# Causal attention inside a two-block layer stack: values as the stationary operand in two column halves, weights normalised before they are transposed

## The reference

```python
for blk in range(s // Q_BLOCK):
    q0, kend = blk * Q_BLOCK, (blk + 1) * Q_BLOCK
    sc = (jnp.einsum('bqhd,bkhd->bhqk', q_nope[:, q0:kend], k_nope[:, :kend])
          + jnp.einsum('bqhd,bkd->bhqk', q_rope[:, q0:kend], k_rope[:, :kend]))
    sc = sc.astype(jnp.float32) * scale
    qi = q0 + jnp.arange(Q_BLOCK)[:, None]
    ki = jnp.arange(kend)[None, :]
    sc = jnp.where(ki <= qi, sc, -jnp.inf)
    pr = jax.nn.softmax(sc, axis=-1).astype(v.dtype)
    outs.append(jnp.einsum('bhqk,bkhd->bqhd', pr, v[:, :kend]))
o = jnp.concatenate(outs, axis=1)
```

## Time and profile before

| | |
|---|---|
| median of 3 runs | 3857.33 us (3854.55 to 3866.11) |
| profiled execution, its own time | 3858.3 us |
| its span | 3856.6 us |
| mean granted TensorE clock | 0.955 of full |
| TensorE matmul busy | 3517.2 us, 91% of the span |
| VectorE / ScalarE / GpSimd busy | 63% / 41% / 29% of the span |
| the attention steps | from 2254 to 2794 us of the span |

### The profile page before, as it was taken

The page is one execution under the profiler, slowest core; times in us unless marked ns, Lnnn a source line. Parts: engine busy times, 40 slices in busy tenths (PEclk is TensorE's granted clock), DMA queues, the critical chain, the costliest instruction groups (busy, mean ns, idle before and its releaser), DMA issues. The chain is left out here.

```text
span 3856.6 us, 44384 instructions
## 1 busy us (share of the span) xinstructions
PE 3517.2 (91%) x16340; PEld 2784.6 (72%) x16340; DVE 2415.6 (63%) x2812; ACT 1580.0 (41%) x2196; POOL 1124.3 (29%) x675
## 2 busy tenths in 40 slices
PE   7899998595999999968989899999989889999998
PEld 3678887464788778756777667777767678878876
DVE  5569557636888888866655222222236488887778
ACT  4322234444777777735222222222232342234443
POOL 1232220234111111143321212222144355545552
PEclk9899999796999999989999999999989999999999
DMA  5312346556999999954421312112154524478854
GB/s 190 108 50 89 115 134 211 211 174 240 374 401 402 398 400 402 367 208 143 144 94 55 126 47 67 58 63 69 44 207 142 175 97 152 155 266 282 270 170 136
DMA packets 225591, 717.22 MB, mean 186 GB/s; under 512 B 26896, under 2 KB 62064, under 8 KB 209296
## 3 DMA queue, kind: packets, MB, share of 16 engines
q1 hardware_dynamic: 184000, 620.37, 44.5%
q10 hardware_dynamic: 31632, 64.80, 4.5%
q0 software_dynamic: 9792, 29.81, 2.0%
HBM read 574.00 MB, written 140.89 MB: 185 GB/s over the span
## 5 line engine op out<-in xcount | busy, mean ns | idle before, releaser
L100 PE MATMUL m_b<-b_high,m_high 128*128 128x512 f32 x960 | 406.0, 423 | 8.4 <-POOL m_low L2616 6.4
L102 PE MATMUL m_b<-b_high,m_low 128*128 128x512 f32 x960 | 383.7, 400 | 0.0
L101 PE MATMUL m_b<-b_rest,m_high 128*128 128x512 f32 x960 | 383.2, 399 | 0.0
L2614 POOL TENSOR_TENSOR m_high<-m_raw,m_one 128x1024 fp32r<-128x1024 f32 x60 | 119.9, 1998 | 782.8 <-PE m_b L102 712.7
L3904 POOL TENSOR_TENSOR t_wl<-t_buf,t_wh 128x512 fp32r<-128x512 f32 x136 | 195.1, 1439 | 240.8 <-ACT t_wh L4035 240.7
L2663 ACT ACTIVATE m_ob<-m_b 128x512 f32<-128x512 f32 x120 | 71.0, 596 | 400.5 <-PE m_b L102 364.8
L100 PE MATMUL zs_z<-zs_hs,zs_high 128*128 128x512 f32 (+1 forms) x584 | 226.5, 388 | 8.5 <-DVE zs_hs L310 8.0
L100 PEld LDWEIGHTS m_b<-b_high,m_high 128*128 128x128 f32 x960 | 185.9, 194 | 61.3 <-issue 12.0
L100 PE MATMUL t_b<-b_high,t_wh 128*128 128x512 f32 x544 | 214.6, 394 | 11.0 <-POOL t_wl L3904 11.0
L101 PEld LDWEIGHTS m_b<-b_rest,m_high 128*128 128x128 f32 x960 | 183.1, 191 | 49.4 <-issue 9.4
L101 PE MATMUL zs_z<-zs_hs,zs_high 128*128 128x512 f32 (+1 forms) x584 | 218.7, 375 | 0.0
(11 more groups left out here) (707 smaller groups left out, 9495.1 us busy)
## 6 DMA issues: line engine op xcount, KB each, us to landing
moe_raw<-in_expert_w SPq DMA_DIRECT2D x79, 2048.0 KB, 10.1
ex_raw<-in_expert_w SPq DMA_DIRECT2D x39, 2048.0 KB, 10.5
t_raw<-in_w_ff SPq DMA_DIRECT2D x192, 256.0 KB, 3.5
m_raw<-in_w_ug SPq DMA_DIRECT2D x60, 512.0 KB, 4.5
t_buf<-hid SPq DMA_DIRECT2D x112, 256.0 KB, 4.4
hid<-t_x SPq DMA_DIRECT2D x96, 256.0 KB, 2.3
yrows<-ex_y ACTq DMA_DIRECT2D x38, 512.0 KB, 11.2
gates<-m_ob SPq DMA_DIRECT2D x32, 512.0 KB, 2.9
```

The source lines that it names most:

```text
L100: nc.tensor.matmul(out, w[0], x[0], start=first, stop=False)
L101: nc.tensor.matmul(out, w[0], x[1], start=False, stop=False)
L102: return nc.tensor.matmul(out, w[1], x[0], start=False, stop=last)
L2614: g.tensor_tensor(W.high[j][:], W.raw[j][:], W.one[:].broadcast_to([P, D]), ALU.mult).then_inc(W.rounded, 1)
```

## The change

Values: the value tile of 64 columns is now the stationary operand and the turned weights move (128 columns). The output has channels on 64 partitions and queries along the row. Even key tiles add into one half of bank 4's partitions, odd key tiles into the other half (`part`, `rows`): two column halves of the array. ScalarE copies the odd half to `at_other` (`copy`), VectorE adds the even half to it into `at_yT`; block 0 has one tile and is only copied, by VectorE. `at_yT` is what is stored, so `pair` and its 32 turns are gone, and the store waits for VectorE's last addition.

Weights: the division by the sum moves ahead of the turns. A new VectorE step `weigh` takes the sum, its reciprocal, and scales `at_pr` in place, up to 128 by 1024. The turns of step n wait for it (`weighed`) and no longer for ScalarE's exponentials alone.

Filler: it is counted in quarters of a unit (2 steps, 6 matmuls): 2, 2, 3, 3, 4, 4, 4, 2 in the blocks of a head and 4 at its end, which is 7 units a head as before. In the state-space mixer each half became two quarters in the same place.

```diff
-        for k in range(KD) if part is None else range(part * KD // 2, (part + 1) * KD // 2):
+        for k in range(KD) if part is None else range(part * KD // 4, (part + 1) * KD // 4):
...
-        self.fills = [2 - b % 2 for b in range(self.QB)]
+        self.fills = [2, 2, 3, 3, 4, 4, 4, 2]
...
+    def rows(self, h):
+        return slice(h % 2 * VH, (h % 2 + 1) * VH)
+
+    def part(self, n, odd):
+
+        return self.ps[4][self.rows(n // self.QB + odd), n % 2 * P:(n % 2 + 1) * P]
...
-        def pair(p):
-            pe.wait_ge(self.taken, 16 * (p + 1))
-            for b in range(self.QB):
-                mm = turn(ps[2 + b // 4][:, b % 4 * P:(b % 4 + 1) * P], self.o[p % 2][:, b], C["ident"][:])
-            mm.then_inc(self.o_turned, 1)
...
-            pe.wait_ge(self.exped, n + 1)
+            pe.wait_ge(self.weighed, n + 1)
             pe.wait_ge(self.moved, self.T0[n])
-            pe.wait_ge(self.o_moved, h // 2 * 2)
...
-            F.halves(pe, self.fills[b])
+            F.quarters(pe, self.fills[b])
             pe.wait_ge(self.moved, self.T0[n + 1])
             pe.wait_ge(self.taken, n)
             for x in range(b + 1):
-                mm = mm_(ps[4][:, n % 2 * P:n % 2 * P + VH], self.pT[n % 2][:, x * P:(x + 1) * P], self.v[:, x, h * VH:(h + 1) * VH], start=x == 0, stop=x == b)
+                mm = mm_(self.part(n, x % 2), self.v[:, x, h * VH:(h + 1) * VH], self.pT[n % 2][:, x * P:(x + 1) * P], start=x < 2, stop=x + 1 >= b)
             mm.then_inc(self.summed, 1)
...
+        def copy(n):
+            if n % self.QB == 0:
+                return
+            act.wait_ge(self.summed, n + 1)
+            act.wait_ge(self.taken, n - 1)
+            S.activation(self.other[n % 2][self.rows(n // self.QB)], self.part(n, 1), ACT.Copy).then_inc(self.copied, 1)
...
             take(self.fills[b])
+            copy(n)
...
+        def weigh(n):
+            b, sm = n % self.QB, self.sm[n % 2]
+            dve.wait_ge(self.exped, n + 1)
+            if b >= 4:
+                st.then(V.tensor_tensor(sm[:, 0:1], sm[:, 0:1], sm[:, 1:2], ALU.add))
+            st.then(V.reciprocal(sm[:, 1:2], sm[:, 0:1]))
+            pr = self.pr[n % 2][:, 0:(b + 1) * P]
+            V.tensor_scalar(pr, pr, sm[:, 1:2], None, ALU.mult).then_inc(self.weighed, 1)
...
             if not last:
                 greatest(n + 1)
+                weigh(n + 1)
...
+            y = self.yT[p % 2][r, b * P:(b + 1) * P]
+            if b:
+                dve.wait_ge(self.copied, n - h)
+                V.tensor_tensor(y, self.part(n, 0), self.other[n % 2][r], ALU.add).then_inc(self.taken, 1)
+            else:
+                V.tensor_copy(y, self.part(n, 0)).then_inc(self.taken, 1)
```

More of the change, by code:

```diff
@@ L2620, in unit @@
     def unit(self, pe, *ms, part=None):
-        for m in ms if part != 1 else ():
+        for m in () if part else ms:
             if m % 2 == 0:
@@ L2642, in multiply, with quarters @@
             self.made += 1
-    def halves(self, pe, count):
-        for x in range(self.parts, min(self.parts + count, 2 * (self.total - self.made))):
-            self.unit(pe, self.made + x // 2, part=x % 2)
+    def quarters(self, pe, count):
+        for x in range(self.parts, min(self.parts + count, 4 * (self.total - self.made))):
+            self.unit(pe, self.made + x // 4, part=x % 4)
             self.parts += 1
     def settle(self):
-        self.made, self.parts = self.made + self.parts // 2, 0
+        self.made, self.parts = self.made + self.parts // 4, 0
     def take(self, act, count=1):
@@ L3068, in tensor @@
                 rows(i + 1)
-            self.F.halves(pe, 1)
+            self.F.quarters(pe, 2)
             pe.wait_ge(self.y_done, i + 1)
@@ L3167, in __init__ @@
         self.pr, self.pT = [q.sb(f"pr{j}", [P, SEQ]) for j in range(2)], [q.sb(f"pT{j}", [P, SEQ]) for j in range(2)]
-        self.o, self.yT = [q.sb(f"o{j}", [P, self.QB, P]) for j in range(2)], q.sb("yT", [P, SEQ])
+        self.other, self.yT = [q.sb(f"other{j}", [P, P]) for j in range(2)], [q.sb(f"yT{j}", [P, SEQ]) for j in range(2)]
         self.mx, self.sm = [q.sb(f"mx{j}", [P, 2]) for j in range(2)], [q.sb(f"sm{j}", [P, 2]) for j in range(2)]
@@ L3268, in tensor @@
                     key(h + 1)
-                if h % 2:
-                    pair(h // 2)
-                F.halves(pe, 2)
+                F.quarters(pe, 4)
                 if h + 1 < MH:
@@ L3316, in weigh, with store @@
             ins.then_inc(self.exped, 1)
[L3318 to L3325, removed]
+        def copy(n):
[4 more added lines that the diff above has]
+            S.activation(self.other[n % 2][self.rows(n // self.QB)], self.part(n, 1), ACT.Copy).then_inc(self.copied, 1)
+        def store(p):
+            act.wait_ge(self.taken, 16 * (p + 1))
+            act.dma_start(self.R["y"][p], self.yT[p % 2][:]).then_inc(self.stored, 16)
         F.take(act, 2)
@@ L3335, in take @@
             begun += parts
-            F.take(act, made + begun // 2 - F.moved)
+            F.take(act, made + begun // 4 - F.moved)
         for n in range(MH * self.QB):
@@ L3347, in scalar @@
             take(self.fills[b])
+            copy(n)
             if last:
-                if h % 2:
-                    pair(h // 2)
-                take(2)
+                take(4)
                 if h + 1 < MH:
@@ L3355, in scalar @@
                         weights(h + 2)
+                if h % 2:
+                    store(h // 2)
     def vector(self, dve):
@@ L3412, in vector @@
         greatest(0)
+        weigh(0)
         for n in range(MH * self.QB):
@@ L3417, in vector @@
                 greatest(n + 1)
+                weigh(n + 1)
             elif h + 1 < MH:
                 query(h + 1)
[L3420 to L3424 removed]
             dve.wait_ge(self.summed, n + 1)
[L3426 removed]
+            p, r = h // 2, self.rows(h)
             if h % 2 == 0 and p >= 2:
[L3428 to L3429 removed]
+                dve.wait_ge(self.stored, 16 * (p - 1))
+            y = self.yT[p % 2][r, b * P:(b + 1) * P]
[4 more added lines that the diff above has]
+                V.tensor_copy(y, self.part(n, 0)).then_inc(self.taken, 1)
             if last and h + 1 < MH:
```

9 lines of the change are left out of this document (2 added, 7 removed).

## The result

The changed kernel takes 3876.1 us (median of 12 runs, 3870.1 to 3881.1 without one run at 5915), the kernel before 3859.5 beside it (12 runs). The ratio is 1.0034 (95% interval 1.0027 to 1.0042): slower by 16.6 us, where 3856 us and no change were forecast. The time lies in the forecast's range, but the forecast's likeliest case is wrong. The profiled execution after took 3871.7 us, its span is 3870.0. In the span the stage of the 64 steps, from the start of the first turn to the last store of `at_yT`, grew from 538.7 us (2254.84 to 2793.58, the latter in the earlier trace rows) to 556.9 (2251.77 to 2808.68), by 18.2.

What follows compares the result with a forecast made beforehand. TensorE's queue bounds the 64 steps (527.4 of 540 us busy). Terms -2.4 - 2.7 - 1.9 + 4.2 + 1.2 = -1.6 us gave 3856 us, counted as no change; range 3842 to 3884 us.

Steps and rivals of the forecast that it cites:

- the forecast's likeliest case: Whole kernel: halves overlap, shape changes cost, inner scalings stay hidden; 3856 us, own range 3846 to 3866, 52%.
- Values: Value matmuls on TensorE: 61.9 us before, 59.5 after including shape changes, so -2.4 us.
- overlap of the halves: Value matmuls: even and odd key tiles run at once, 0.22 us a pair, 35.2 us for 160 pairs.
- price of the shape: Each step's switch between whole-array work and 64-column value tiles: 0.38 us in and out, 64 times, 24.3 us.
- Rivals 1 to 3: Value matmuls: no overlap but shape price, +24.3, 20%; overlap without price, -26.7, 13%; neither, 3858 us, 10%.
- Turns that go and the end: Dropped output turns: -2.7 us in TensorE's queue; shorter chain from last value matmul to store: -1.9 us.
- The scaling at head starts: Before each head's first turn, without filler cover: scaling lengthens the chain by 0.52 us, eight times, +4.2 us.
- GpSimd against the scaling: Scaling waits while GpSimd splits a tile: 0.3 us at four head starts, +1.2 us; elsewhere hidden under filler and values.
- The bound of 1.3: Inner blocks: a scaling's wait for GpSimd is up to 1.3 us, taken from one example in the earlier trace.
- Rival 4: GpSimd's second operation precedes the waiting scaling: block 4 in odd heads 1.5 us late, four head starts 2.4; +15.6, 5%.
- about 17 us, in eight places: Sign: TensorE's idle time before the turns after the change, released by VectorE.
- the bound of 552 us: Sign: the forecast is wrong if the steps take over 552 us (or under 525) instead of 538.

Runs made afterwards that it cites:

- e7: Kernel of e1 with all value matmuls of a block in one column half: 3880.1 us, 1.004 of the kernel before.
- e9: Kernel of e1 with a filler quarter moved inside each value group from three key tiles on, 48 more tile shape changes: 3882.4 us, 1.0051 of before.
- e2: Changed kernel without the sum's addition, reciprocal and scaling, output not divided by the sums: 3844.9 us, 0.9955 of before.
- e1: Changed kernel with the small addition of two sums done as a reduction over two columns: 3852.7 us, 0.9975 of before.
- e5: Changed kernel with the small addition as a TENSOR_SCALAR, one tensor and one scalar operand: 3854.1 us, 0.9969 of before.
- e4: Kernel of e1 with filler quarters dealt as before the change (4,2,4,2,4,2,4,2): 3883.7 us, 1.0049 of before.
- e8: Kernel of e1 with filler split around every head's first scores, the very first included, and one more quarter before block 1's turns: 3835.9 us, 0.9929 of before.
- e10: Kernel before the change with filler split around every head's first scores, the very first included: 3843.9 us, 0.9954 of before.
- e11: Kernel of e8 again, unedited, in more rounds: 3835.7 us, 0.9931 of before.
- e12: Changed kernel again, unedited, in the same rounds as e11: 3878.2 us, 1.0046 of before.

## Why the prediction was wrong

**Values: mechanism right, saving too small.** The overlap of the halves and the price of the shape both came as forecast. Block 7 of head 3 after the change (load track and matmul track, the key projection behind), against the earlier trace rows:

```profile
2527.20 0.85 PEld L3263 LDWEIGHTS m_b<-at_pT,at_v 128*64 128x64 f32 x16 [0.37 <-issue]
2527.20 1.09 PE L3263 MATMUL m_b<-at_pT,at_v 128*64 128x128 f32 x16
...
2528.23 0.30 PEld L3215 LDWEIGHTS m_b<-at_ckv,at_wk 128*128 128x128 f32 x2 [0.17 <-issue]
```

The load track idles 0.37 us going in and 0.17 coming out. e7 prices the overlap at 27.8 us (forecast 26.7), e9 a switch amid filler at 0.37 (forecast 0.38). By start times (from a group's first start to the next group's), the value groups before took 60.7 us, not 61.9. In e2 they take 44.5, the filler ahead of them 7.6 more and the turns behind 2.7 more: 54.8, and less 35.2 for 160 pairs that leaves 19.6 us for 64 switches, 0.31 each. The term took 0.38, from a switch between other groups. A switch whose way out leads to turns cost less here (0.31) than e9's, which lead to filler of 512 columns (0.37). The term is -5.9 instead of -2.4. Rivals 1 to 3 are out.

**Turns that go and the end: right.** The groups of turns and what stood around them gave 3.2 (forecast 2.7). The end of the steps after the change, against the earlier trace rows:

```profile
2807.99 0.27 ACT L3321 ACTIVATE at_other<-m_b 64x128 f32<-64x128 f32 x1 [0.44 <-PE m_b L3263]
2808.36 0.29 DVE L3439 TENSOR_TENSOR at_yT<-m_b,at_other 64x128 f32<-64x128 f32 x1 [4.56 <-ACT at_other L3321]
2808.68 0.33 ACTq L3325 DMA_DIRECT2D y<-at_yT  x1
```

0.7 us from the copy to the store. From the start of the last value matmul's last record to the store it is 1.02 us, and was 2.97: 2.0 less (forecast 1.9).

**The scaling at head starts: right.** Eight starts cost 4.4 us more; 4.2 were forecast, and 1.2 for GpSimd. (The wait before was 1.40 in seven of them and 2.24 in the first, not 1.40 in eight.) Of the 1.2 only 0.3 came: in four heads the scaling of 128 columns starts 0.27 us before `m_high` ends, as forecast, but takes 0.35 instead of 0.28, so it loses 0.07. Wider scalings show the same: one that starts inside a GpSimd operation loses what is left of it, less about 0.2 us (0.55 left and 0.35 lost for 512 columns; 2.18 left and 1.98 lost for 768).

**GpSimd against the scaling: the step that failed.** It priced one operation of VectorE against GpSimd, the scaling, and held the wait ("up to 1.3") to lie under the cover. There are two that wait, and between them a reciprocal that does not. The small addition loses 0.5 us in block 4, 1.6 in block 5, 1.4 in block 6 and 1.2 in block 7; the reciprocal lets `m_low` in; the scaling loses 2.0 each time. Against these 2.5, 3.6, 3.4 and 3.1 us stand covers of 0.9, 2.2, 1.9 and 1.8, and what is left is 1.3 to 1.5 us, 15 times, 21.4 us. The bound of 1.3 was itself no bound: it is what happened to be left of one GpSimd operation in the one example, where the scaling lost 1.1 (1.85 for 0.75). In that example, in the earlier trace rows, VectorE went in between GpSimd's two, and nothing stood between that would let GpSimd pass; it is what e1 restores. Rival 4 had GpSimd win the second turn, with 5%. One of its two places came at its size, block 4 in odd heads (1.54 us, four times, for 1.5), though by way of the addition, of which it knew nothing; its other place, the head starts, did not, and the eleven waits in blocks 5, 6 and 7 it did not name. The Trainium skill's rule on two SBUF inputs, quoted under e5, and line 3406 in the trace of before were to be had; the prediction counted line 3414 at its 0.15 us alone.

**What was missing: the clock, and the end of a matmul.** The prediction counted a wait once, at its length. Two things came on top, the 4.2 us of busy time. First, the clock: from the first turn of one head to that of the next it is 71.3 us in heads 1 and 5 of the changed kernel and 72.9 in head 3, where the clock fell to its lower level. A fall costs 1.6 us, and the two together 3.1. Second, a turn that does not wait starts 0.07 us before the last value matmul is over: from the first value matmul of block 5 to the last one's end it is 0.88 us in the heads with a wait behind it, and to the turn's start 0.81 in the others. 15 times that is 1.1 us. e4 fits the same two prices: seven falls and 20 more waits give 12.4 us of its 12.5.

When does the clock fall? Shown is this. In the eleven profiles in which the first head's turns wait for 2.2 or 2.8 us, the kernel before among them, it falls there; in the three in which that wait is covered (e8, e10, e11) it does not. Behind the first head it falls in after, e12, e4 and e9, and in none of the other ten. In e1 and e5 the waits at head starts are as long as in after, so their length alone does not decide; after, e12 and e4 have more waits around them, and e9 has more changes of shape instead. What decides which wait it falls behind stays open.

**The sum as measured.** -5.9 for values, -3.2 and -2.0 for turns and end, -0.2 for scores, +4.4 at head starts, +21.4 inside the heads, +3.1 for the clock, +1.1 for the ends of matmuls: +18.7. The first head's 0.5 of the 4.4 lies ahead of the stage, which begins with the first turn: 18.2, as the stage has it, and 16.6 in the medians. The step that failed makes 21.4 us of it, and 25.6 with the 4.2 that came on top; without it the stage would be 7.4 us shorter than before, as it is in e1.

Of what was to show it: 0.055 apart, 0.37 us in and 0.17 out, 2.0 less at the end came; "about 17 us, in eight places" came as 37.8 in 23; the bound of 552 us was passed by 5. The chances do not quite add up either: rivals 1 and 4, the slower ones, have 25% between them, and "slower" was given 22%.

## What to carry to other kernels

When work moves onto a chain that filler barely covers, list every instruction of that chain, however small, and ask of each whether it waits for another engine: an addition of 0.15 us with two SBUF inputs, met by GpSimd in 15 of 32 places, cost 23 us, and a reduction in its place cost nothing. Look at the order too: here an instruction that doesn't contend, between two that do, handed the turn back. And count idle time of TensorE at more than its length where the clock can fall behind it; a filler cut in two around the exposed scores was worth more (11 us of the stage, in either kernel) than the change itself (8 us, e10 against e11).

## What the runs showed of the hardware

- Issued while GpSimd was splitting a tile, a TENSOR_TENSOR on 128 by 1 with two SBUF inputs waited in 15 of 15 places in after, up to 1.63 us (and 0.28 in the four of before). TENSOR_REDUCE on two columns (0.155), RECIPROCAL (0.16) and a TENSOR_SCALAR of one column (0.21) never did. The scaling, a TENSOR_SCALAR of 128 to 1024 columns from SBUF to SBUF, lost what was left of the GpSimd operation less about 0.2 us, 2.05 us at most (e11).
- Two column halves of 64 run fully in parallel in float32 (0.055 us between record starts against 0.113 in one half), as the row halves of the earlier trace rows do (0.059).
- Changing from a 128 wide to a 64 wide tile and back costs 0.31 to 0.37 us.
- A fall of the clock to its lower level amid these steps cost 1.6 us (head 3 of after against heads 1 and 5).
- The same program in two executions had its clock fall behind different waits, with the same waits to 0.1 us.
